# Hybrid diffusion block: the convolution stage of the SSD mixer with a longer bank cycle, earlier weight splits and later transposes

## What is computed

```python
proj = jnp.concatenate([hc, hx], axis=1) @ w_in
z, xbc, dt_raw = jnp.split(proj, [SSD_INNER, SSD_INNER + SSD_CONV_DIM], axis=-1)
xbc = silu(concat([dw_conv(xbc[:, :Lc]), dw_conv(xbc[:, Lc:])]))   # 5 taps, per channel
xs, bm, cm = jnp.split(xbc, [SSD_INNER, SSD_INNER + SSD_GROUPS * SSD_STATE], axis=-1)
dt = softplus(dt_raw + dt_bias)
# ssd_chunked, both directions: cumulated sums of dt*A, C times B, states, outputs
```

## Time and profile before

| | us |
|---|---|
| median of 3 runs (lowest to highest) | 1235.91 (1235.59 to 1236.2) |
| the profiled execution's own time | 1236.16 |
| its span, first to last instruction | 1234.4 |
| PE busy (share of the span) | 1159.1 (94%) |
| DVE, ACT, POOL busy | 878.1, 623.3, 217.3 |
| mean granted TensorE clock | 0.984 |

### The profile page before, as it was taken

The page is one execution under the profiler, slowest core; times in us unless marked ns, Lnnn a source line. Parts: engine busy times, 40 slices in busy tenths (PEclk is TensorE's granted clock), DMA queues, the critical chain, the costliest instruction groups (busy, mean ns, idle before and its releaser), DMA issues.

```text
span 1234.4 us, 19406 instructions
## 1 busy us (share of the span) xinstructions
PE 1159.1 (94%) x6954; PEld 970.9 (79%) x6954; DVE 878.1 (71%) x1340; ACT 623.3 (50%) x1056; POOL 217.3 (18%) x162
## 2 busy tenths in 40 slices
PE   5799999888999999999999879998999899999996
PEld 3577676678988888888888868886677799999996
DVE  0896888976787777776665588885988756666654
ACT  3646888734532222232222556447677456666642
POOL 0201445422100000000111100004777200000010
PEclk9899999999999999999999989999999899999999
DMA  9534132240465655564452132321212344555572
GB/s 381 193 121 135 52 103 87 69 164 8 171 224 186 203 189 170 186 211 162 162 166 67 58 103 87 100 85 35 79 59 68 103 137 164 171 176 170 165 216 65
DMA packets 48176, 168.23 MB, mean 136 GB/s; under 512 B 5232, under 2 KB 6512, under 8 KB 47856
## 3 DMA queue, kind: packets, MB, share of 16 engines
q1 hardware_dynamic: 48112, 167.38, 41.2%
HBM read 166.31 MB, written 1.05 MB: 136 GB/s over the span
## 4 chain that ended last, share of the span: by engine, by line
PE 65%; DVE 18%; ACT 9%; issue 5%; DMA 1%; POOL 1%; DVEq 0%; ACTq 0%; SPq 0%
PE bank L1737 19%; PE bank L1739 19%; PE bank L1738 19%; DVE scratch L1479 5%; DVE w_lo L1108 3%; ACT w_hi L609 2%; PE bank L2164 2%; DMA ada_start<-in_ada_w 1%; PE bank L2197 1%; ACT scratch L914 1%; DVE softmax_max L1279 1%; PE bank L2176 1%; ACT conv_in L911 1%; PE bank L2186 1%; DVE mla_h_lo L1299 1%
## 5 line engine op out<-in xcount | busy, mean ns | idle before, releaser
L1108 DVE TENSOR_TENSOR w_lo<-raw,w_hi 128x1024 fp32r<-128x1024 f32 (+1 forms) x226 | 277.1, 1228 | 133.4 <-ACT w_hi L609 133.2
L609 ACT ACTIVATE w_hi<-raw 128x1024 fp32r<-128x1024 f32 (+1 forms) x226 | 230.3, 1021 | 240.8 <-PE bank L1739 217.7
L1737 PE MATMUL bank<-ffn_h_lo,w_hi 128*128 128x258 f32 (+2 forms) x736 | 246.0, 334 | 5.7 <-DVE ffn_h_lo L1382 2.3
L1739 PE MATMUL bank<-ffn_h_hi,w_lo 128*128 128x258 f32 (+2 forms) x736 | 244.5, 332 | 0.0
L1738 PE MATMUL bank<-ffn_h_hi,w_hi 128*128 128x258 f32 (+2 forms) x736 | 244.4, 332 | 0.0
L1737 PEld LDWEIGHTS bank<-ffn_h_lo,w_hi 128*128 128x128 f32 x736 | 139.4, 189 | 21.9 <-DVE ffn_h_lo L1382 2.7
L1738 PEld LDWEIGHTS bank<-ffn_h_hi,w_hi 128*128 128x128 f32 x736 | 139.2, 189 | 14.5
L1739 PEld LDWEIGHTS bank<-ffn_h_hi,w_lo 128*128 128x128 f32 x736 | 138.9, 189 | 14.7
L465 POOL TENSOR_TENSOR scratch<-scratch 128x512 f32<-128x512 f32 (+1 forms) x24 | 34.1, 1419 | 618.3 <-ACT scratch L618 618.3
L1737 PE MATMUL bank<-ssd_h_lo,w_hi 128*128 128x256 f32 (+2 forms) x360 | 126.0, 350 | 12.4 <-DVE w_lo L1108 10.1
L1737 PE MATMUL bank<-ffn_hidden_lo,w_hi 128*128 128x256 f32 (+1 forms) x374 | 123.6, 330 | 1.0 <-DVE ffn_hidden_lo L1691 0.9
(11 more groups left out here) (275 smaller groups left out, 2185.6 us busy)
## 6 DMA issues: line engine op xcount, KB each, us to landing
raw<-in_w SPq DMA_DIRECT2D x120, 512.0 KB, 4.3
scratch<-in_vec_w SPq DMA_DIRECT2D x56, 512.0 KB, 3.5
vec_weights<-in_vec_w SPq DMA_DIRECT2D x24, 512.0 KB, 3.6
raw<-in_w_xbc SPq DMA_DIRECT2D x24, 512.0 KB, 3.5
ada_start<-in_ada_w SPq DMA_DIRECT2D x8, 1024.0 KB, 17.2
raw<-in_w_z SPq DMA_DIRECT2D x16, 512.0 KB, 3.5
raw<-in_w_so SPq DMA_DIRECT2D x16, 512.0 KB, 3.6
raw<-in_w SPq DMA_DIRECT2D x16, 384.0 KB, 4.5
```

The costliest lines, as they stand in the source:

```text
L609: A(wh[s % RING][:, 0:c], raw[s % RING][:, 0:c], ACT.Copy).then_inc(w_hi, 1)
L1108: V.tensor_tensor(wl[s % RING][:, 0:c], raw[s % RING][:, 0:c], wh[s % RING][:, 0:c].bitcast(f32), SUB).then_inc(w_lo, 1)
L1737: mm(o, lh, rl, start=first, stop=False)
L1739: return mm(o, ll, rh, start=False, stop=final)
```

## The change

- x tiles go round four banks (5, 6, 7, 0); tile t waits for the copy of tile t-4.
- Step 0 on ACT and DVE splits blocks 4 to 7 of the B and C weights at once (DVE two of them before its taps), step 1 the dt block, step t from 2 on the x (later z) block that stands six conv tiles ahead.
- The transposes of tile t stand behind conv tile t+3 on PE (before t+2), those of tiles 21, 22 and 23 behind z tiles 0, 1 and 2.
- Their copies to `B_tok` and `x_tok` move from DVE to ACT, behind the SiLU of tile t+2.
- C times B moves behind tile 14, the transposes of dt behind tile 11, the cumulated sums behind tile 19; the masks of C times B on DVE go behind step 15, the state weights behind step 21. `z_out(0)` goes into ACT's step 22. The banks of these products change.
- The hardware loops of the stage on ACT, DVE and PE are written out; `par` columns are addressed directly.
- POOL waits for `conv_y` 24 as well before its first weighing.

```diff
-CB_BANK = (7, 0)
+CB_BANK = (1, 4)
+X_BANK = (5, 6, 7, 0)
...
+def conv_bank(t):
+    return X_BANK[t % 4] if t >= 8 else C_BANK[t - 4] if t >= 4 else (0, 1, 4, 5)[t]
+def conv_block(t):
+    return BC + t if t < 8 else XS + t - 8
+def conv_splits(t):
+    if t == 0:
+        return [BC + n for n in range(4, 8)]
+    if t == 1:
+        return [DT]
+    return [ZS + 3] if t == 22 else [XS + t - 2] if t < 21 else []
...
             pool.wait_ge(w6_done, 3)
+            pool.wait_ge(conv_y, 24)
             pool.wait_ge(conv_ev, 20)
...
-            def conv(t, n, s, u, kind):
+            def z_out(t):
+                act.wait_ge(w_used, ZS + t + 1)
+                A(zs[:, t, :], bank[z_bank(t)][:, 0:LAT], ACT.Copy).then_inc(z_cp, 1)
+                hi(ZS + t + 4, ZS + t + 4)
+            def conv(t):
+                kind, u, o = "BCxxxx"[t // 4], t % 2, bank[conv_bank(t)]
                 seg = slice(1, 2) if kind == "C" else slice(0, 2)
-                o = bank[2 + t if kind == "B" and t >= 2 else C_BANK[t - 4] if kind == "C" else u]
-                act.wait_ge(w_used, n + 1)
-                if late(t, 2):
+                act.wait_ge(w_used, conv_block(t) + 1)
+                if t >= 2:
                     act.wait_ge(conv_tap, 4 * t - 4)
                 if kind == "C":
                     A(up[:, u, 1, 2:258], o[:, 256:512], ACT.Copy).then_inc(conv_up, 1)
...
                     A(up[:, u, :, 2:258], o[:, :].rearrange("p (s t) -> p s t", s=2), ACT.Copy).then_inc(conv_up, 1)
                 act.wait_ge(conv_up, t + 1)
                 acc = T[:, u, :].rearrange("p (s t) -> p s t", s=2)[:, seg, :]
-                A(acc, up[:, u, seg, 0:256], ACT.Identity, bias=par[:, ds(PAR["conv_b"] + t, 1)],
-                  scale=par[:, ds(PAR["conv_w"] + 5 * t, 1)]).then_inc(conv_init, 1)
-                hi(n + 4, s + 4)
+                A(acc, up[:, u, seg, 0:256], ACT.Identity, bias=par[:, PAR["conv_b"] + t:PAR["conv_b"] + t + 1],
+                  scale=par[:, PAR["conv_w"] + 5 * t:PAR["conv_w"] + 5 * t + 1]).then_inc(conv_init, 1)
+                for n in conv_splits(t):
+                    hi(n, n)
                 act.wait_ge(conv_tap, 4 * t + 4)
-                if kind == "x":
-                    act.wait_ge(conv_tr, max(4, t - 5) if isinstance(t, int) else t - 5)
-                if kind == "B" and t >= 2:
-                    act.wait_ge(conv_tr, t - 1)
                 if kind == "C":
                     A(CT[:, t - 4:t - 3, :], acc, ACT.Silu).then_inc(conv_y, 1)
                     return
+                if kind == "x":
+                    act.wait_ge(conv_tr, t - 5)
+                elif t >= 2:
+                    act.wait_ge(conv_tr, t - 1)
                 y = T[:, 2 + u, :].rearrange("p (s t) -> p s t", s=2)[:, seg, :]
                 A(y, acc, ACT.Silu).then_inc(conv_y, 1)
                 if kind == "B":
                     act.wait_ge(conv_y, t + 1)
                     A(BT[:, t, :], T[:, 2 + u, 256:512], ACT.Copy).then_inc(bt_cp, 1)
+            def to_tokens(t):
+                src = bank[2 + t % 2][:, :].rearrange("p (t n) -> p t n", n=128)
+                if t < 4:
+                    act.wait_ge(conv_tr, t + 1)
+                    A(Bt[:, :, t, :], src, ACT.Copy).then_inc(conv_ev, 1)
+                else:
+                    act.wait_ge(conv_tr, t - 3)
+                    A(xtok[:, :, 128 * (t - 8):128 * (t - 8) + 128], src, ACT.Copy).then_inc(conv_ev, 1)
...
             for t in range(8):
-                conv(t, BC + t, BC + t, t % 2, "BC"[t // 4])
+                conv(t)
+                if 2 <= t < 6:
+                    to_tokens(t - 2)
             act.wait_ge(w_used, DT + 1)
             A(dtT[:, :], bank[4][0:64, :], ACT.Copy).then_inc(dt_cp, 1)
-            hi(DT + RING, DT + RING)
             V_ = dtw
-            conv(8, XS, XS, 0, "x")
-            act.wait_ge(dt_dve, 2)
-            A(V_[:, 2, :], V_[:, 1, :], ACT.Exp, scale=-1.0).then_inc(dt_act, 1)
-            A(rows[:, 64:128], rows[:, 64:128], ACT.Exp).then_inc(dt_act, 1)
-            conv(9, XS + 1, XS + 1, 1, "x")
-            act.wait_ge(dt_dve, 3)
-            A(V_[:, 4, :], V_[:, 3, :], ACT.Ln).then_inc(dt_act, 1)
-            for u in range(2, 4):
-                conv(8 + u, XS + u, XS + u, u % 2, "x")
-            with act.Fori(1, 4) as i:
-                for u in range(4):
-                    conv(8 + 4 * i + u, XS + 4 * i + u, XS + u, u % 2, "x")
-            act.wait_ge(cum_mm, 1)
-            A(et[:, :], bank[6][:, 0:384], ACT.Exp).then_inc(cum_exp, 1)
-            def z_out(t):
-                act.wait_ge(w_used, ZS + t + 1)
-                A(zs[:, t, :], bank[z_bank(t)][:, 0:LAT], ACT.Copy).then_inc(z_cp, 1)
-                hi(ZS + t + 4, ZS + t + 4)
+            for t in range(8, 24):
+                conv(t)
+                if t == 9:
+                    act.wait_ge(dt_dve, 2)
+                    A(V_[:, 2, :], V_[:, 1, :], ACT.Exp, scale=-1.0).then_inc(dt_act, 1)
+                    A(rows[:, 64:128], rows[:, 64:128], ACT.Exp).then_inc(dt_act, 1)
+                if t >= 10:
+                    to_tokens(t - 2)
+                if t == 10:
+                    act.wait_ge(dt_dve, 3)
+                    A(V_[:, 4, :], V_[:, 3, :], ACT.Ln).then_inc(dt_act, 1)
+                if t == 20:
+                    act.wait_ge(cum_mm, 1)
+                    A(et[:, :], bank[4][:, 0:384], ACT.Exp).then_inc(cum_exp, 1)
+                if t == 22:
+                    z_out(0)
...
-            z_out(0)
             z_out(1)
-            act.wait_ge(dt_dve, 12)
+            to_tokens(22)
             mask_backward(0)
             z_out(2)
+            to_tokens(23)
             z_out(3)
...
+            for t in range(12, 24):
+                conv(t)
+                if t == 15:
+                    dve.wait_ge(cb_mm, 2)
...
+                if t == 21:
+                    dve.wait_ge(cum_exp, 1)
...
-            def conv_tile(t, n, s, u, kind):
-                if late(t, 8):
-                    pe.wait_ge(conv_up, t - 1)
+            def conv_tile(t):
+                n = conv_block(t)
+                if t >= 12:
+                    pe.wait_ge(conv_up, t - 3)
                 elif t >= 6:
-                    pe.wait_ge(conv_up, t - 5)
-                u = C_BANK[t - 4] if kind == "C" else u
-                c = slice(CTX, TOK) if kind == "C" else slice(0, TOK)
-                tile(n, s, bank[u][:, c], lambda k: H1h[:, k, c], lambda k: H1l[:, k, c], 0, 8, True, True).then_inc(w_used, 1)
-            def to_tokens(t, u, r):
+                    pe.wait_ge(conv_up, (1, 2, 4, 5, 6, 7)[t - 6])
+                c = slice(CTX, TOK) if t < 8 else slice(0, TOK)
+                tile(n, n, bank[conv_bank(t)][:, c], lambda k: H1h[:, k, c], lambda k: H1l[:, k, c], 0, 8, True, True).then_inc(w_used, 1)
+            def to_tokens(t):
+                r = t if t < 4 else t - 4
+                u = t % 2
                 pe.wait_ge(conv_y, t + 1)
-                if late(r, 2):
+                if r >= 2:
                     pe.wait_ge(conv_ev, r - 1)
                 for k in range(4):
                     last = nc.tensor.transpose(bank[2 + u][:, 128 * k:128 * k + 128], T[:, 2 + u, 128 * k:128 * k + 128], tabv("ident"))
                 last.then_inc(conv_tr, 1)
...
-            for t in range(4, 8):
-                conv_tile(t, BC + t, BC + t, t % 2, "C")
-                to_tokens(t - 4, t % 2, t - 4)
+            conv_tile(4)
+            conv_tile(5)
+            to_tokens(0)
+            conv_tile(6)
+            conv_tile(7)
+            to_tokens(1)
+            pe.wait_ge(conv_up, 3)
...
+            to_tokens(2)
+            conv_tile(8)
+            to_tokens(3)
+            for t in range(9, 24):
+                conv_tile(t)
+                if t >= 11:
+                    to_tokens(t - 3)
+                if t == 11:
+                    pe.wait_ge(dt_cp, 1)
+                    for q in range(4):
+                        last = nc.tensor.transpose(bank[4][:, 64 * q:64 * q + 64], dtT[:, 128 * q:128 * q + 128], tab[0:64, 0:64])
+                    last.then_inc(dt_tr, 1)
+                if t == 14:
+                    c_times_b()
+                if t == 19:
+                    cumulated()
...
+            pe.wait_ge(cum_exp, 1)
+            pe.wait_ge(conv_up, 21)
             z_tile(0)
-            to_tokens(22, 0, 18)
-            to_tokens(23, 1, 19)
-            for t in range(1, 4):
-                z_tile(t)
+            to_tokens(21)
+            z_tile(1)
+            to_tokens(22)
+            z_tile(2)
+            to_tokens(23)
+            z_tile(3)
+            pe.wait_ge(conv_up, 24)
```

More of the change, by code:

```diff
@@ L1501, in _ @@
             V.scalar_tensor_tensor(V_[:, 1, :], V_[:, 0, :], -1.0, V_[:, 0, :], MUL, ALU.max).then_inc(dt_dve, 1)
[L1502 removed]
+            conv(10)
             dve.wait_ge(dt_act, 1)
@@ L2108, in _ @@
             last.then_inc(w_used, 1)
```

(25 more changed lines are left out.)

93 lines of the change are left out of this document (45 added, 48 removed).

## The result

The changed kernel takes 1243.95 us in the median (1242.62 to 1244.16), the kernel before 1236.06 (1235.59 to 1236.98): ratio 1.0061, 95% interval [1.0046, 1.0076], 7.9 us **slower**, a small loss (0.6%) but clear of the interval. The forecast was 1237.0, and its range ended at 1240.4. The profiled execution took 1243.99 us, against 1236.16.

A forecast was written before the change was run, and what follows sets the result against it. TensorE, 94% busy, bounds the kernel, and POOL's mask sets the decay of pair 2. From the 1235.91 us median, +0.5 late decay and +0.6 slow clock, +1.1 in all, gave 1237.0 us; range 1233.2 to 1240.4.

The forecast's parts named there:

- Part 1: Start of the stage: earlier splits remove 8.3 us of `w_lo` waits, but copy 8 comes 1.2 us later, at 742.7.
- Parts 2 and 3: Steps 9 to 13 and the middle: tile 12 near 748.8, tile 15 about 770.5, z tile 0 at 828.
- Part 4: End of the stage: copy 23 at 839.6, 3.9 us later than before; first decay at 851.3, 2.0 us ahead.
- Part 5: POOL's lead-in: starts at 851.3, 6.7 us later, slack spent; decay of pair 2 at 874.2, 0.5 us later.
- the sum: Whole kernel: +0.5 us late decay and +0.6 us slow clock make +1.1 us, 1237.0 us against the median.
- POOL's factor: Stretch of POOL's 18.65 us chain up to its third mask, taken as 1.23, giving 22.9 us.
- the mask of 871.32: POOL's mask in the kernel before, 2.34 us for 1.90; its 1.23 was applied to POOL's whole chain.
- The slow clock: Behind PE's wait of some 3 us at the decay of pair 2: 0.6 us, not quite half of 1.4.
- What comes after 880: Behind the decay of pair 2: PE runs gapless some 90 us, so earlier gains or losses count one for one.
- The second: Between last `x_tok` copy and decay pair 2: POOL and DVE block each other, +4.7 us, 1240.6; chance 0.25.
- agrees only in part: Port rule against POOL's rows before: weighings stretched 1.64 times, a backward product at 869.46 not at all.

The follow-up runs named there:

- experiment 7: The kernel before with the early splits alone (blocks 4 to 7 in step 0, dt in step 1, x blocks in steps 2 to 5): 1237.35 us, ratio 1.0002.
- experiment 4: The changed kernel with four unused float32 matmuls on PE ahead of the decay of pair 2, in its wait for POOL: 1240.74 us, ratio 1.0034.
- experiment 1: The changed kernel with ACT's last x token copy moved ahead of the eight backward masks and z copy 2: 1235.01 us, ratio 0.9986.
- experiment 3: The kernel before with POOL also waiting for the copy of z tile 2 before its first weighing: 1240.16 us, ratio 1.0025.
- experiment 6: The changed kernel with ACT's token copies ahead of its wait for the taps, last copy still behind the masks: 1236.71 us, ratio 0.9996.
- experiment 12: The kernel before with three unused matmuls on PE ahead of its last diagonal, in the 3.34 us wait: 1235.44 us, ratio 0.9991.

## Why the prediction was wrong

*Part 1, right.* Copy 8 was foretold for 742.7. It came at 743.17, which is 742.68 when the 0.49 us lost before the stage are taken off. That the early splits are worth nothing at the end is what experiment 7 shows, ratio 1.0002.

*Parts 2 and 3, right.* With the 0.49 taken off: tile 12 at 748.96 (foretold 748.8), tile 15 at 770.27 (770.5), z tile 0 at 828.03 (828).

*Part 4, right.* Copy 23 at 839.82 (839.6), first decay at 851.39 (851.3), POOL's start at 851.46 (851.3). The rows of these and of the next part, ACT's timeline:

```profile
743.17 0.58 ACT L940 ACTIVATE conv_in<-bank 128x512 f32<-128x512 f32 x1
...
840.31 0.60 ACT L940 ACTIVATE conv_in<-bank 128x512 f32<-128x512 f32 x1
...
847.64 2.44 ACT L1008 ACTIVATE h_space<-tab,dtA 128x128 f32<-128x128 f32 x8
...
851.20 0.59 ACT L969 ACTIVATE x_tok<-bank 128x512 f32<-128x512 f32 x1
```

The copy that POOL waited for is the last row, 3.6 us behind the masks' start, though its transposes had ended on PE at 846.83.

*Part 5 and the sum: where it failed, in three places.* The sum put POOL's lateness at 0.5 us, the slow clock at 0.6 and all that comes later at 0; they were 2.0, 2.7 and 2.6 (0.5 more lies before the stage, within what executions differ by there).
- **POOL's factor.** "I take the factor of the mask of 871.32 (1.23)": 22.9 us. The stretch took 24.2, a factor of 1.30, so the decay stood at 875.73 after correction and not at 874.2. A factor was the wrong form. POOL's rows show steps: five of them, which had to let a 1024-wide instruction of DVE with two SBUF inputs pass, are longer by 0.97 us (2.87 for 1.90, 4.02 for 3.05), and two that met 512-wide ones by 0.5. That is 5.8 us in rows, which overlap a little: 5.6 in the chain. This takes the 24.2 us apart; it was not tested as a forecast.
- **The slow clock.** "I count not quite half of it, 0.6." It was 2.67 (experiment 4). The nearest row showed 1.4 for 2.56 us of idle time, and the forecast wait was 3 us; halving it had no row behind it. The clock doesn't fall in proportion: experiments 1 and 3 waited 1.66 and 2.2 us there and lost nothing, after and experiment 6 waited 4.11 and lost 2.7 and 1.5.
- **What comes after 880.** The sum said that whatever stands at that decay "goes into the total one for one". It doesn't: 2.0 + 2.7 us at the diagonal became 6.8 at the FFN.

*The rivals.* The second, POOL and DVE in each other's way, had the right side, and it said that it decides from a factor of 1.3 on, which is the one measured. That its size at the diagonal, 3.3 + 1.4 = 4.7 us, is the measured 2.0 + 2.7 = 4.7 is luck: one term was too large by what the other lacked. DVE's timeline beside POOL's product of 870.89 and its mask of 873.29 shows how it goes:

```profile
871.50 2.92 DVE L1144 TENSOR_TENSOR w_lo<-raw,w_hi 128x1024 fp32r<-128x1024 f32 x1
874.34 2.91 DVE L1622 TENSOR_TENSOR h_space<-decay,scratch 128x1024 f32<-128x1024 f32 x1
...
886.16 1.22 DVE L1144 TENSOR_TENSOR w_lo<-raw,w_hi 128x1024 fp32r<-128x1024 f32 x1
```

The split issued at 871.50 ends 1.09 us after POOL's product (873.33), POOL's mask ends 1.7 us after that split, and the `h_space` product ends 1.1 us after the mask (876.16): each comes through when the other is done. The split of 886.16, which came first, takes its 1.22, and POOL's next mask, issued at 886.18, takes 2.96 for 1.90. That is the rule of the Trainium skill (SBUF — State Buffer, Who interferes with whom): the first holds, the other blocks. The trace agrees. The prediction took the rule to mean that POOL loses every meeting, and read the rows as "agrees only in part" since the product of 869.46 was not stretched. But that product came first, and the one that waited was DVE's, with 1.61 us for 0.69:

```profile
870.29 1.61 DVE L1585 TENSOR_TENSOR y_tok<-y_tok,scratch 128x512 f32<-128x512 f32 x1
```

What decides is who comes first. Even this rival ended at 1240.6, 3.4 us under the measured time, since the later clock was in no case. The windows of before at 976 to 984, shown with experiment 12, lay there to be read, and the range should have had room for them.

## What to carry to other kernels

When an edit moves a copy to another engine, look at what stands ahead of the *last* such copy in that engine's order, and who waits for all of them: here one copy behind eight masks cost some 9 us (4.4 of them at the decay, the rest slow clock), and moving it up a few lines, or making the waiter ask only for its own part, gave it back. The lead won on the bound engine was worth nothing here, since another engine's start wasn't won with it, and it cost: the wait grew to 4.1 us, and the clock fell behind it. Where the wait can't be shortened, matmuls with no purpose in it kept the clock up (2.7, 3.1, 2.6 and 1.5 us in the profiles), but check behind the next wait whether the fall only moved there.
